# Rows of x fetched as 8 KB runs in five transfers, and the repeated turns left out

## What is computed

```python
h_p = jnp.concatenate([meta, x_prompt], axis=1); h_s = x_sample
xn = rmsnorm(h, p['g_mix'])          # x * rsqrt(mean(x*x) + EPS) * g
proj = xn @ p['w_in']                # q, k, v, r, a_low, u
...                                  # gated linear attention on q, k, v, r; S5 on u
h = h + mixed @ p['w_out']
h = h + hier_moe(rmsnorm(h, p['g_ffn']), ...)   # 32 experts, top 1 group, top 2 experts
```

## Time and profile before

| | before |
|---|---|
| median of 3 runs | 1576.11 us (1575.69 to 1579.9) |
| span of the profiled execution | 1574.4 us |
| median less span | 1.7 us |
| PE busy | 1295.5 us, 82% |
| DVE / ACT / POOL busy | 30% / 16% / 6% |
| mean rate of the transfers | 309 GB/s |
| chain that ended last, by engine | PE 55%, DMA 39%, DVE 3%, issue 2% |

### The profile page before, as it was taken

The page is one execution under the profiler, slowest core; times in us unless marked ns, Lnnn a source line. Parts: engine busy times, 40 slices in busy tenths (PEclk is TensorE's granted clock), DMA queues, the critical chain, the costliest instruction groups (busy, mean ns, idle before and its releaser), DMA issues.

```text
span 1574.4 us, 18035 instructions
## 1 busy us (share of the span) xinstructions
PE 1295.5 (82%) x7188; PEld 716.5 (46%) x7188; DVE 469.3 (30%) x1012; ACT 254.0 (16%) x681; POOL 93.6 (6%) x256
## 2 busy tenths in 40 slices
PE   7999999999999998868658669569659758756877
PEld 6667777766578885314214224224214214213322
DVE  5387576243520005303103103102202102201314
ACT  4452323452221111200000000000000000000012
POOL 7800000100010002000000000000000000000000
PEclk9999999999999999879879779878888788877968
DMA  9333133350389642999999999999999999999996
GB/s 218 109 108 103 58 108 107 81 163 32 107 286 394 247 156 86 427 427 429 427 428 428 428 428 428 428 428 426 427 428 425 427 429 423 426 422 412 387 426 239
DMA packets 114039, 486.62 MB, mean 309 GB/s; under 512 B 18308, under 2 KB 86216, under 8 KB 86584
## 3 DMA queue, kind: packets, MB, share of 16 engines
q1 hardware_dynamic: 111208, 475.71, 75.7%
q0 software_dynamic: 2480, 9.98, 1.9%
q10 hardware_dynamic: 288, 0.04, 0.0%
HBM read 478.42 MB, written 10.78 MB: 311 GB/s over the span
## 4 chain that ended last, share of the span: by engine, by line
PE 55%; DMA 39%; DVE 3%; issue 2%; SPq 1%; ACT 1%; POOLq 0%; POOL 0%; ACTq 0%; DVEq 0%
DMA arena<-in_w_up 38%; PE ps L2122 20%; PE ps L2356 11%; PE ps L2186 7%; PE ps L2301 4%; PE ps L2395 2%; PE ps L2190 2%; PE ps L2268 1%; PE ps L2057 1%; DVE arena L1728 1%; PE ps L1992 1%; PE ps L1980 1%; PE ps L2378 1%; SPq L558 1%; DMA arena<-in_x_prompt 1%
## 5 line engine op out<-in xcount | busy, mean ns | idle before, releaser
L2356 PE MATMUL ps<-arena 128*32 128x512 f32 x2048 | 308.6, 748 | 191.3 <-DMA arena<-in_w_up 189.8
L2122 PE MATMUL ps<-arena 128*128 128x336 f32 (+1 forms) x1152 | 328.3, 442 | 0.0
L2356 PEld LDWEIGHTS ps<-arena 128*32 128x32 f32 x2048 | 78.1, 133 | 412.4 <-issue 411.6
L2122 PEld LDWEIGHTS ps<-arena 128*128 128x128 f32 x1152 | 215.3, 190 | 95.9 <-issue 3.7
L2395 PE MATMUL ps<-arena 128*32 128x512 f32 x1024 | 150.3, 740 | 20.7 <-DVE arena L1751 19.8
L1743 DVE COPY arena<-ps 128x512 f32<-128x512 f32 x31 | 21.3, 688 | 387.9 <-PE ps L2356 387.9
L1171 ACT ACTIVATE arena<-ps 128x128 f32<-128x128 f32 x32 | 8.9, 277 | 692.4 <-PE ps L2378 692.4
L2186 PE MATMUL ps<-arena 128*128 128x256 f32 x512 | 114.4, 382 | 0.0
L2301 PE MATMUL ps<-arena 128*128 128x512 f32 (+3 forms) x192 | 106.9, 688 | 6.6 <-DVE arena L1728 4.7
L2186 PEld LDWEIGHTS ps<-arena 128*128 128x128 f32 x512 | 96.0, 190 | 14.1 <-issue 1.2
L1728 DVE TENSOR_TENSOR arena<-arena,ps 128x1024 f32<-128x1024 f32 (+1 forms) x48 | 58.4, 1218 | 115.7 <-PE ps L2301 115.7
(11 more groups left out here) (395 smaller groups left out, 976.6 us busy)
## 6 DMA issues: line engine op xcount, KB each, us to landing
arena<-in_w_down SPq DMA_DIRECT2D x61, 2048.0 KB, 21.3
arena<-in_w_gate SPq DMA_DIRECT2D x60, 2048.0 KB, 18.5
arena<-in_w_up SPq DMA_DIRECT2D x60, 2048.0 KB, 23.1
arena<-in_w_in SPq DMA_DIRECT2D x15, 2048.0 KB, 9.1
arena<-in_w_out SPq DMA_DIRECT2D x8, 2048.0 KB, 8.3
arena<-in_w_gate SPq DMA_DIRECT2D x8, 1024.0 KB, 16.1
arena<-in_w_up SPq DMA_DIRECT2D x8, 1024.0 KB, 18.2
arena<-in_w_down SPq DMA_DIRECT2D x6, 1024.0 KB, 20.3
```

The lines of the kernel that those rows point to most:

```text
L2122: mm = te.matmul(o, w, x, start=(k == 0), stop=(k == kt - 1))
L2356: mm = te.matmul(ps[CAP * x:CAP * x + CAP, 0, :], xT[:, 4 * q + at, CAP * i:CAP * i + CAP], wpiece[4 * (q // 2) + 2 * up + q % 2][:, HID * ...
```

## The change

Each piece of x is one transfer with runs of 8 KB, a whole row. The two pieces of sample rows are one, so that x comes in five transfers (twelve `dma_start` calls before). The semaphore values that ACT and TensorE wait for follow from the number of transfers of each tile. `repeat_turns` and its call are gone. Nothing else is changed.

```diff
-XW = 256
...
             def load_rows(dst, src, t):
-                for b in range(2):
-                    d_, s_ = (v.rearrange("r (a b w) -> r a b w", b=2, w=XW)[:, :, b] for v in (dst, src))
-                    sp.dma_start(d_, s_).then_inc(x_loaded[t], 16)
+                sp.dma_start(dst, src).then_inc(x_loaded[t], 16)
...
-            load_rows(xr[48:96, 2, :], xs[0:48, :], 2)
-            load_rows(xr[96:112, 2, :], xs[48:64, :], 2)
+            load_rows(xr[48:112, 2, :], xs, 2)
...
             def square(t):
-                act.wait_ge(x_loaded[t], (64, 32, 96)[t])
+                act.wait_ge(x_loaded[t], (32, 16, 32)[t])
...
-            def repeat_turns(count):
-                for k in range(count):
-                    te.transpose(ps[:, 7, 0:XT_ROWS], xr[:, 1, k % KT:D:KT], ident[0:XT_ROWS, 0:XT_ROWS])
...
-                pe.wait_ge(x_loaded[t], (64, 32, 96)[t])
+                pe.wait_ge(x_loaded[t], (32, 16, 32)[t])
...
                 mm.then_inc(xn_turned, 1)
-                if n == 7:
-                    repeat_turns(20)
```

## The result

| | before | after |
|---|---|---|
| median of 12 runs | 1572.07 us (1569.55 to 1579.9) | 1584.82 us (1577.12 to 1590.95) |
| ratio | | 1.007, interval 1.005 to 1.0089 |
| span of the profiled execution | 1574.4 us | 1584.4 us |
| its own time | | 1586.19 us |
| front: the spreading of the norm factors ends | 23.41 us | 24.96 us |

The account below looks back on a forecast made before the run. It took the first 23 us as on the path, with DVE's sequence the new bound: spreading at 19.6 instead of 23.41, gain 3.8 less 0.1 for unseen waits, 1576.1 - 3.7 = 1572.4 us; range 1571.0 to 1577.6.

Parts of the forecast that it names:

- DVE's sequence: Front: DVE's work on x's tiles becomes the bound, spreading ends at 19.6, 3.8 us earlier; as main case, chance 0.43.
- the 16 named as the point from which it decides: Arrival of x: if tile 2 lands later than about 16 us, under 215 GB/s, the slower case decides.
- the 11.5 of the sum: Arrival of x: tile 2 was expected at 11.5 us, in place of 17.6.
- I take 2.0 and 1.0: Small loads on ACT's queue: assumed delays behind x's longer packets, 2.0 us for g_mix and 1.0 for lam_im.
- The bound of 2.5: Small loads: g_mix at most 2.5 us later, 8 rows to an engine each waiting for one 0.31 us packet.
- if g_mix lands after 9.3: Sign of being wrong: from 9.3 us on, each further microsecond of g_mix's landing delays the whole sequence.
- I take 330: Arrival of x: assumed rate of 330 GB/s, between the weight chunk's and the slower x window's.
- The bound at 190: Arrival of x: slowest rate considered, 190 GB/s, at which a tile takes 4.8 us, no gain.
- Rival 2: First projection tile: TensorE's clock is low there, costing 1.0 to 2.8 us; gain only 1.8, 1574.3 us; chance 0.24.
- The repeated turns: TensorE's front: 2.57 us taken out, only about 1.0 of it real delay; they may have bought the clock.
- rival 4: Tile 2's turns and first projection tile: x arrives as before, clock stays low; 0.8 to 3.1 us slower, 1577.7; chance 0.13.
- The 1576.1: Base of the sum: before's median time in us, from which the forecast gain was subtracted.

Follow-up runs that it names:

- e8: After with TensorE's own code for the overflow rounds, loop and jump left out: 1571.37 us, ratio 0.9996.
- e12: After with small loads issued ahead of x on SyncE's queue, the repeated turns kept, no overflow rounds in TensorE's list: 1569.54 us, ratio 0.9966.
- e17: Small loads first, x replaced by three transfers of 128 contiguous 8 KB rows of w_up; one run, 1575.44 us.
- e18: As e17, but with 112 rows to a transfer; one run, 1568.31 us.
- e6: After with the repeated turns back and the small loads issued by SyncE ahead of x instead of by ACT: 1573.52 us, ratio 1.0.
- e14: e6 with 20 turns of the identity added at the start of TensorE's list: 1571.17 us, ratio 0.996.
- e5: After with 20 turns of the identity at the start of TensorE's list, where it waits anyway: 1576.97 us, ratio 1.0011.
- e2: Before with only the 20 repeated turns left out, x still in 1 KB runs: 1585.6 us, ratio 1.0053.
- e13: After with 40 turns of the identity at the start of TensorE's list: 1573.07 us, ratio 0.998.
- e4: Before with 40 no-operations meant for TensorE's start, which the build dropped, so before once more: 1576.54 us, ratio 0.9997.

## Why the prediction was wrong

**What held.** The first 23 us are on the path, and what is lost there carries on one for one (24.96 - 23.41 = 1.55, and 1.5 at 434 and 630 us; the fourteen executions up to 1431; e8 against e12). SyncE's five x issues are over at 3.32, within the forecast 2.8 to 4.8. DVE's sequence was the new bound, as said, and x was not: tile 2 landed at 2.65 + 13.1 = 15.8, just under the 16 named as the point from which it decides, though far from the 11.5 of the sum.

**The small loads: right mechanism, a size four times too small.** This is the term "I take 2.0 and 1.0". Measured g_mix + 7.5 us (13.65 against 6.1) and lam_im + 4.6. The bound of 2.5 multiplied 8 rows by one x packet each. The one packet each was right. Two things were not: the packet, priced at 0.31 us from the rate of the weight stream, took 0.52 in the records (0.31 is what it takes in e17's transfers of 128 rows, so this is the miss on x's rate once more), and the loads ahead in the same queue were priced for ACT alone, though g_mix can't start before they have gone through; that was 3.8 of the 7.5. So the bound of the unknown was no bound. The prediction had the warning in it (wrong "if g_mix lands after 9.3"), and the queue's order in front of it. By the Trainium skill (DMA: Bandwidth & Descriptors, Queues, rings and completion order) an engine takes a whole packet of some 9 to 17 descriptors from one ring before it turns to the next; g_mix's 8 rows to an engine would then pass in one turn. The trace disagrees: they are spread over 4.4 us.

**The rate of x: wrong.** "I take 330", between two rates of the trace; it was 141 to 289. The step took the length of the runs for what x and the weights differ in. They also differ in rows per transfer, 112 against 128, and e17 against e18 shows that this is it. The bound at 190 held, except for the window 10 to 12 at 141. In this kernel it cost nothing, since g_mix was later still; in e6 and e14, with g_mix out of the way, x is the bound.

**DVE's sequence.** From the first part to the end of the last turns 16.6 - 8.3 = 8.3 us were forecast, 20.88 - 13.67 = 7.2 measured. Tile 0 took 3.1 us in place of 4.4 (the square, at 11.73, was under way before g_mix came), tile 1 took 3.0 in place of 3.3, and the last turns behind it 1.1 in place of 0.6. **The clock.** Rival 2 is what happened: 0.56 and 0.50 in the windows 16 to 22, and 3.42 us for the 8 instructions, 1.15 more than at full speed. Together: 19.6 + 5.4 (g_mix at 13.67 in place of 8.3) - 1.1 + 1.15 = 25.0, the measured 24.96. So the front's error is mostly that of one term. The prediction also weighed a rule of the Trainium skill (TensorE: Matmul & The Clock Gate, Part 4: PE-mode transpose), that turns don't count towards the higher clock in the same way; e5's rows disagree, since the clock rose with nothing but turns behind it.

**The repeated turns: the missing term.** The prediction priced their 2.57 us and their hold on the clock. In before's order of loads leaving them out makes the front 1.7 to 2.5 us later (e2), where the step saw 1.0 us to be had; the slow turns and the slow first tile, as rival 4 had described them, were the larger side. This is the step that failed: it put everything else about 20 fewer turns at nothing, without a reason. The list is shorter, and at a jump 1400 us later the fetch of TensorE's program takes 19.9 us in place of 8.3. This is most of the loss: the medians are 12.75 us apart, the fronts 1.8 (mean of three executions, 24.96, 23.80 and 25.65, against two, 23.41 and 22.58), a list of before's length or longer gives the time back (e5, and e13 with a front of 24.37), leaving out the turns alone loses it (e2), and without the jump after is at before's time (e8). No rival had it. Rival 4, the slow side, looked for its price in x and the clock, 1.6 us. An "issue" piece of 8.31 us stood in the chain of before; the prediction's rows of that chain end at 50 us.

**The base.** The 1576.1 from which the sum started was the median of three runs, and the profile was of an execution whose last products took 8.83 us in place of 7.13; nine more runs put the median at 1572.07. That is chance in the runs and no part of the loss.

**What stays open.** Why the extra fetches come with a shorter list, in most executions and not in all, and what fills the time between two of them. Why the last round's products run at a lower clock in some executions. And what makes the transfers of 112 rows slow. The 0.95 us between 630 and 1434 need no cause of their own: from the front's end to 1431 two executions of before's program (before and e4) differ by 1.75 us.

## What to carry to other kernels

Issue small loads that gate an engine ahead of the large ones, on the same queue: beside a stream of long rows each small row waits for one long packet, and the small loads of a queue wait in a row. Count rows per transfer before run length: 112 rows of 8 KB ran at 258 to 266 GB/s, 128 at 389 to 422. When an edit changes the number of instructions, price it by a run with the length put back, and look in the chain of both kernels for long "issue" pieces, above all where the program steps over a block that doesn't run; such a wait can outweigh all that was meant.

## What the runs showed of the hardware that was not expected

- Program fetches of 16 KB share the transfer engines with the weights. At 414 GB/s of weights the next fetch began up to 6.2 us after the one before it; waits of 7.9 to 8.6 us had one or two, those of 19.9 four or five.
- The long runs depend on the list's length as a share of executions: 24 of 36 runs above 1581 us with 20 turns fewer, 13 of 176 with before's number (11 of them before itself), none of 36 with 20 more.
- 64 B packets on one queue and 8 KB packets on the other alternate about one by one (0.55 us for each small one, 0.52 us for an 8 KB packet of x).
- An 8 KB packet takes 0.31 us in transfers of 128 rows (e17) and 0.50 in transfers of 112 (e18).
- The granted clock, 0.50 (1.2 GHz) while TensorE worked through turns, reached 1.00 in e5 before any product had run. Near the end of the kernel the same 16 products take 7.13 us in some executions and 8.82 or 8.83 in others (granted clock 1.00 and 0.83 in after and before), which splits the profiled executions with a short wait into those up to 1574.7 us and those from 1575.4.
